# Forgetting attention in a kernel of two transformer blocks: value products gathered per pair of heads, four rounds of turned tiles, an uneven filling list

## The reference

```python
logits = einsum('bhqd,bhkd->bhqk', qh[start:end], kh[:end]) * scale
logits = logits + cum[start:end, None] - cum[None, :end]      # cum: running sum of log-sigmoid gates
p = softmax(where(causal, logits, -inf))
outs.append(einsum('bhqk,bhkd->bhqd', p, vh[:end]))
```

## Time and profile before

| | |
|---|---|
| median of 3 runs | 1869.99 us (1869.86 to 1870.62) |
| profiled execution, its own time | 1870.26 us |
| span of the profiled execution | 1868.5 us |
| PE busy | 1858.9 us, 99% of the span |
| granted PE clock | 1.00 over the span |
| `x_stage`, first score to last value product | 1335.9 to 1483.8 us of the span |

### The profile page before, as it was taken

How to read it: one execution, slowest core, us unless ns; L and a number is a source line. 1 busy time by engine, 2 the same in 40 slices (tenths; PEclk the granted TensorE clock), 3 DMA queues, 4 the chain that set the end, 5 groups by cost and what they waited for, 6 DMA issues and landing times.

```text
span 1868.5 us, 24518 instructions
## 1 busy us (share of the span) xinstructions
PE 1858.9 (99%) x9034; PEld 1499.5 (80%) x9034; DVE 1186.3 (63%) x1828; ACT 803.2 (43%) x1215; POOL 152.2 (8%) x111
## 2 busy tenths in 40 slices
PE   9999999999999999999999999999999999999999
PEld 7777888888887788888888887888777788888887
DVE  5686676356647866763576498675666667644762
ACT  5475443233436754332344343422577554322341
POOL 1132000000021020000000101121210010000000
PEclk9999999999999999999999999999999999999999
DMA  6211222322231122323322322445333222223223
GB/s 220 85 52 68 90 97 83 112 91 104 77 109 49 69 69 93 110 68 113 106 89 85 115 90 93 147 137 186 126 127 113 69 90 90 86 94 113 90 79 101
DMA packets 39521, 185.99 MB, mean 100 GB/s; under 512 B 4448, under 2 KB 5856, under 8 KB 24848
## 3 DMA queue, kind: packets, MB, share of 16 engines
q1 hardware_dynamic: 39152, 184.77, 29.0%
q10 hardware_dynamic: 288, 0.16, 0.0%
HBM read 176.42 MB, written 8.49 MB: 99 GB/s over the span
## 4 chain that ended last, share of the span: by engine, by line
PE 93%; DVE 4%; ACT 2%; issue 1%; DMA 1%; POOL 0%; SPq 0%; DVEq 0%; ACTq 0%; POOLq 0%
PE banks L771 55%; PE banks L1320 22%; PE banks L818 5%; PE banks L1234 1%; PE banks L1259 1%; PE banks L1245 1%; PE banks L1368 1%; DVE w_lo L2056 1%; PE banks L1397 1%; DVE tmp L2436 1%; ACT w_hi L1474 1%; PE banks L1380 1%; PE banks L1333 1%; PE banks L991 1%; PE banks L1130 0%
## 5 line engine op out<-in xcount | busy, mean ns | idle before, releaser
L771 PE MATMUL banks<-xn_hi,w_hi 128*128 128x512 f32 x1208 | 467.2, 390 | 0.5 <-DVE big L2154 0.5
L771 PE MATMUL banks<-xn_hi,w_lo 128*128 128x512 f32 x1208 | 466.1, 389 | 0.0
L771 PE MATMUL banks<-xn_lo,w_hi 128*128 128x512 f32 x1208 | 466.0, 389 | 0.0
L1474 ACT ACTIVATE w_hi<-raw 128x2048 fp32r<-128x2048 f32 (+2 forms) x134 | 228.3, 1704 | 226.8 <-PE banks L771 188.9
L2056 DVE TENSOR_TENSOR w_lo<-raw,w_hi 128x2048 fp32r<-128x2048 f32 (+2 forms) x134 | 273.5, 2041 | 48.5 <-ACT w_hi L1474 48.0
L771 PEld LDWEIGHTS banks<-xn_hi,w_hi 128*128 128x128 f32 x1208 | 226.8, 188 | 49.0 <-issue 1.4
L771 PEld LDWEIGHTS banks<-xn_lo,w_hi 128*128 128x128 f32 x1208 | 226.8, 188 | 47.4 <-issue 0.5
L771 PEld LDWEIGHTS banks<-xn_hi,w_lo 128*128 128x128 f32 x1208 | 226.8, 188 | 47.1
L1540 ACT ACTIVATE tmp<-scaled_h,par 128x512 f32<-128x512 f32 x132 | 100.5, 809 | 349.8 <-DVE scaled_h L2112 349.8
L2112 DVE TENSOR_TENSOR scaled_h<-banks,token_rs 128x512 f32<-128x512 f32 x132 | 85.0, 686 | 183.3 <-PE banks L771 166.0
L1320 PE MATMUL banks<-xn_hi,w_hi 128*128 128x512 f32 x400 | 161.2, 403 | 0.6 <-DVE big L2162 0.6
(11 more groups left out here) (302 smaller groups left out, 2646.3 us busy)
## 6 DMA issues: line engine op xcount, KB each, us to landing
raw<-weights SPq DMA_DIRECT2D x114, 1024.0 KB, 4.9
raw<-weights SPq DMA_DIRECT2D x24, 768.0 KB, 4.3
raw<-weights SPq DMA_DIRECT2D x24, 640.0 KB, 3.9
big<-scratch SPq DMA_DIRECT2D x40, 256.0 KB, 4.5
att<-scratch SPq DMA_DIRECT2D x16, 256.0 KB, 3.9
scratch<-stage SPq DMA_DIRECT2D x12, 256.0 KB, 4.6
scratch<-con SPq DMA_DIRECT2D x12, 256.0 KB, 2.2
raw<-weights SPq DMA_DIRECT2D x4, 512.0 KB, 3.7
```

Of the source, the lines that this page charges most:

```text
L771: return pe.matmul(psum[:, 2 * p + m, :], w[:, at_:at_ + P], x_part(k), start=start, stop=stop)
L1474: act.activation(w_hi[:, sl], raw[:, sl], ACT.Identity).then_inc(hi_done, 1)
```

## The change

The value products of a pair's three rounds are no longer issued one round per step. `values(it)` does all three rounds of a pair at once, at the end of the steps g = 3*it + 4 (4, 7, ..., 25), that is behind the next pair's second round. Since turned tiles must live longer, they get slots for four rounds, not two: the two further ones lie in the upper half of the buffer `xn_hi`, which this stage does not use otherwise. The waits on `f_pv` count pairs, not rounds. The filling list is no longer even: 13 matmuls in each of the steps 0 to 3, then 6, 14, 14 six times (6 in the steps that hold value products), then 4, 10, 10, 8. The sum is 288 as before.

```diff
-X_FILL = weave([("S_OUT", 4), ("X_OUT", 2)], [12] * 22 + [6] * 4)
+X_FILL = weave([("S_OUT", 4), ("X_OUT", 2)], [13] * 4 + [6, 14, 14] * 6 + [4, 10, 10, 8])
...
+        late_slots = at("late_slots", 4 * T, offset=xn_at + 4 * T * 4)
...
         def f_slot(m, r):
-            return chunk(big, 16 + 2 * (r % 2) + m)
+            return chunk(big, 16 + 2 * (r % 4) + m) if r % 4 < 2 else chunk(late_slots, 2 * (r % 4 - 2) + m)
...
-                def values(r):
-                    it = r // 3
-                    if r % 3 == 0:
-                        pe.wait_ge(f_v, it + 1)
-                        if it:
-                            pe.wait_ge(f_out, it)
-                    pe.wait_ge(f_copied, 2 * r + 2)
-                    for i, col, w in f_blocks(r):
+                def values(it):
+                    pe.wait_ge(f_v, it + 1)
+                    if it:
+                        pe.wait_ge(f_out, it)
+                    pe.wait_ge(f_copied, 2 * (3 * it + 3))
+                    for r in range(3 * it, 3 * it + 3):
+                        for i, col, w in f_blocks(r):
...
                     last.then_inc(f_pv, 1)
...
-                    if g >= 2:
-                        values(g - 2)
+                    if g >= 4 and g % 3 == 1:
+                        values((g - 4) // 3)
...
-                    act.wait_ge(f_pv, 3 * (it - 1))
+                    act.wait_ge(f_pv, it - 1)
...
-                        if m == 0 and r >= 2:
-                            act.wait_ge(f_pv, r - 1)
+                        if m == 0 and r >= 4:
+                            act.wait_ge(f_pv, (r - 4) // 3 + 1)
...
-                    act.wait_ge(f_pv, 3 * it + 3)
+                    act.wait_ge(f_pv, it + 1)
```

More of the change, by code:

```diff
@@ L178, in blocks_program @@
         x = at("x", DC * T)
+        xn_at = place[0]
         xn_hi, xn_lo = at("xn_hi", DC * T, F32R), at("xn_lo", DC * T, F32R)
@@ L1246, in turn @@
                         last.then_inc(f_pt, 1)
-                def values(r):
-                    it = r // 3
-                    if r % 3 == 0:
-                        pe.wait_ge(f_v, it + 1)
-                        if it:
-                            pe.wait_ge(f_out, it)
-                    pe.wait_ge(f_copied, 2 * r + 2)
-                    for i, col, w in f_blocks(r):
[L1256 to L1261, removed]
+                def values(it):
[5 more added lines that the diff above has]
+                        for i, col, w in f_blocks(r):
+                            for j in range(i + 1):
+                                for m in range(2):
+                                    at_ = j * P + 64 * m
+                                    last = pe.matmul(psum[64 * m:64 * m + 64, 0, i * P:(i + 1) * P], f_vtok[it % 2][:, at_:at_ + 64],
+                                                     f_slot(m, r)[:, col + j * P:col + (j + 1) * P],
+                                                     start=(i == 0), stop=(i == 3 and j == 3), skip_group_check=True)
                     last.then_inc(f_pv, 1)
```

## The result

The changed kernel takes 1878.04 us (median of 6 runs, 1874.71 to 1879.22) against 1870.10 before (1869.86 to 1870.62). The ratio of the runs compared is 1.0037, 95% interval 1.0026 to 1.0047: slower, by some 5 to 9 us. The forecast was 1875.0 with a range of 1872.0 to 1877.5; the sign and the mechanism held. The median of the six lies 0.5 us above the range; by the ratio of the runs compared the time is 1877.0, within it.

What follows compares the result with a forecast made beforehand. PE, busy 99% of the span, was taken as the bound. Stalls of 7.4 us less 2.4 saved by tile shape gave +5.0, so 1869.99 became 1875.0 us, range 1872.0 to 1877.5.

Steps and rivals of the forecast that it cites:

- The bound: In this stage PE is busy 99%, its issue is paid in full; DVE and ACT, 73 and 75% busy, cannot follow at once.
- the waits of steps 10, 13, 17, 18 and 22: PE stalls on DVE's and ACT's queues: 2.1, 0.4, 0.4, 2.8, and 2.5 in step 22, 1.3 more than before.
- The saving by shape: Value products: 16 rounds no longer standing alone save one tile-shape change of 0.15 each, 2.4 us.
- The rival without a saving: Value products: the 0.15 is paid per round for new operands, so nothing is saved: +7.4, 1877.4 us; chance 6%.
- Step 4: The second weight slab now begins in step 3, so PE stalls 0.4 us in step 4, as at step 13.
- Step 7's 0.3: Step 7: no slab is split in the step before, so maxima are done in time; no stall.
- The upper bound: High end of the range of change: 5.0 + 1.5 for the long stalls + 0.8 for less shape saving, +7.3 us.
- the three waits of 0.4: Short PE stalls in steps 4, 13 and 17, 0.4 us each; they may be nothing (-1.2) or double.
- The clock: Rival: a 2.8 us wait of PE halves its clock over the next step: +11 us, 1881; chance 4%.
- PE's waits of step 22 did not change it: Argument against a clock fall: in the kernel before, step 22's waits left the granted clock at 1.00.
- if the clock leaves 1.00: One of two signs of being wrong; the other was PE showing no wait in steps 10 and 18.
- Half of it: Rival: one of the two large stalls, step 10 or 18, falls away: +2.2 to +2.9, 1872.5 us; chance 15%.

Runs made afterwards that it cites:

- the kernel with steps 20 to 25 aligned: The changed kernel with 12, 12, 12, 8, 8, 8 filling matmuls in steps 20 to 25, not 14, 14, 4, 10, 10, 8: 1874.79 us.
- the kernel with steps 17 to 19 aligned: The changed kernel with 10, 12, 12 filling matmuls in steps 17, 18, 19 in place of 14, 14, 6: 1874.05 us.
- a fitted one: The changed kernel with its filling list replaced by one fitted to the roads read from the trace: 1867.04 us, ratio 0.9982 to the kernel before.

## Why the prediction was right, and where it was off

**The bound.** That PE's stream is paid in full and that DVE's and ACT's roads have a fixed length held: roads read off the trace of before gave the waits of steps 10, 13, 17, 18 and 22 to within 0.1 us (2.1, 0.4, 0.4, 2.8 and 2.5 forecast; 2.1, 0.4, 0.4, 2.7 and 2.5 measured).

**The saving by shape.** 2.4 forecast, 2.5 measured (2.33 in place of 2.64 a pair of heads). The rival without a saving is out.

**Step 4.** The term "the same pattern as at step 13: stall 0.4" was mis-sized: 1.1. The DVE row ahead of it is this, beside the POOL row that runs in the same time:

```profile
1350.31 2.49 POOL L742 TENSOR_TENSOR tn<-big 128x512 f32<-128x512 f32 x2 [9.30 <-DMA big<-scratch]
...
1351.82 2.06 DVE L2295 TENSOR_TENSOR w_lo<-raw,w_hi 128x1024 fp32r<-128x1024 f32 x1
...
1361.82 0.29 PE L1226 MATMUL banks<-mask_b,ident_b 128*128 128x128 bf16 x2 [0.94 <-DVE small L2719]
```

In the kernel with steps 20 to 25 aligned, whose list is the same up to step 19, POOL is through a little earlier relative to DVE, the row is short, and the mask of step 4 waits 0.25 by the bracket, not 0.94 (0.4 and 1.1 from start to start):

```profile
1351.17 1.04 POOL L742 TENSOR_TENSOR tn<-big 128x512 f32<-128x512 f32 x1
...
1352.68 1.21 DVE L2295 TENSOR_TENSOR w_lo<-raw,w_hi 128x1024 fp32r<-128x1024 f32 x1
...
1361.83 0.28 PE L1226 MATMUL banks<-mask_b,ident_b 128*128 128x128 bf16 x2 [0.25 <-DVE small L2719]
```

The longer row, 0.85 us, delays everything behind it on DVE, and 0.7 of it arrive in the wait. Step 7's 0.3, forecast as nothing, is the same sort. In the changed kernel DVE's L2739 takes 1.54 us beside POOL's L742:

```profile
1377.18 1.04 POOL L742 TENSOR_TENSOR tn<-big 128x512 f32<-128x512 f32 x1 [13.25 <-DMA big<-scratch]
1377.23 1.54 DVE L2739 TENSOR_TENSOR tn_r<-tn,more_r 128x512 fp32r<-128x512 f32 x1 [1.85 <-ACT more_r L1945]
```

In the kernel with steps 17 to 19 aligned, the same program up to there, POOL comes later, the row is short, and step 7 has no wait:

```profile
1377.76 0.69 DVE L2739 TENSOR_TENSOR tn_r<-tn,more_r 128x512 fp32r<-128x512 f32 x1 [1.84 <-ACT more_r L1945]
...
1378.40 1.04 POOL L742 TENSOR_TENSOR tn<-big 128x512 f32<-128x512 f32 x1 [13.91 <-DMA big<-scratch]
```

The kernel before has such a meeting too, where PE does not wait:

```profile
1400.63 1.06 POOL L740 TENSOR_TENSOR tn<-big 128x512 f32<-128x512 f32 x1 [4.87 <-PE banks L916]
...
1400.71 2.06 DVE L2294 TENSOR_TENSOR w_lo<-raw,w_hi 128x1024 fp32r<-128x1024 f32 x1
```

The Trainium skill ("SBUF — State Buffer", section "Who interferes with whom") says that a DVE instruction with two SBUF inputs contends with a GpSimd instruction that reads SBUF; both of these DVE instructions have two, and these rows agree.

**The upper bound.** The text on bounds says that the three waits of 0.4 may double, but the sum for the high end, 5.0 + 1.5 + 0.8, leaves this 1.2 out. With it the high end is +8.5, some 1878.5. Step 4 used 0.7 of it.

**The clock.** It was a rival at 4% and +11 us, 6 of them for the clock; it came in 4 of 6 runs, and by the prediction's own sign of being wrong ("if the clock leaves 1.00") it was wrong in this. The sum has no term for it, and the step that failed is "PE's waits of step 22 did not change it": from start to start those were 1.2 us in all, and the changed kernel's, with the fall behind them, are 2.5. The sort of condition was right, its place (step 18) was not the one of this profile, its chance was too low and its price too high: the fall in the profile cost 1.7. With the 1.0 that steps 4 and 7 have over the forecast, these 1.7 are the whole distance of the profiled run from 1875.0. The other three runs of the second group are not traced. They lie up to 4.5 us above the two at 1.000; a mean of 0.998 goes with two falls in the trace of the kernel with steps 17 to 19 aligned, and two would cost some 3.4 (an estimate, twice the 1.7). Up to 2.4 us of a run then stay open. The Trainium skill ("TensorE: Matmul & The Clock Gate", section "HAM oscillation — how this bites in real kernels"), cited there, names pauses between bursts as what brings the clock to half; the traces agree in sort, and here the falls followed waits of 2.3 to 2.7 us within one step. The mean was 1.000 in all 44 runs of the four kernels whose waits in the stage are 0.6 us or less each as idle time. Between them lie the grouped kernel with the even list (2.0 in step 22; 3 of 11 runs at 0.999) and the kernel before with the new list (2.0 in step 18; 2 of 8). These runs, and the one of the kernel before, have no trace, so where their clock fell is not shown.

**Half of it.** The rival in which one of the two large waits falls away did not happen: both were there to 0.1 us.

## What to carry to other kernels

When filling work is moved between the steps of a software pipeline, count what each other engine has queued between two hand-overs to the bound engine, not its share of busy time: here DVE was 27% idle and still made PE wait in every step whose own work fell under the length of that queue. Unit ends matter as much as amounts, because a bank is emptied at a fixed place of the next step. The grouping that saves changes of tile shape (0.15 us each here) gained only with a list that keeps every such road covered: by itself it broke even, with the wrong list it lost 8 us, with a fitted one it gained 3.5.

## What the runs showed of the hardware that was not expected

- In three traces the granted clock fell to 0.50 after waits of PE that came to only 2.3 to 2.7 us in a step, at three different places, and by the mean clocks only in part of the executions of one and the same program. While it was low, 40 value instructions took 4.00 us in place of 2.33.
- A DVE subtraction of 128x1024 took 2.06 us in place of 1.21 and one of 128x512 1.54 in place of 0.69 when POOL was reading at the same time. Executions of programs that are the same up to there differ in whether the two meet. What makes POOL come earlier or later is not shown: its wait before the meeting ended on the DMA into `big` in two of the cases above, and on PE in one.
